# Softmax attention loop of a three-block transformer step: probabilities scaled before the transpose, values stationary, output written transposed

## What is computed

```python
def causal_attention_blocks(q, k, v):        # q, k: (1, 8, 256, 96), v: (1, 8, 256, 64); Q_BLOCK = 128
    for i in range(S // Q_BLOCK):
        s = jnp.einsum('bhqd,bhkd->bhqk', q[:, :, lo:hi], k[:, :, :hi])
        p = jax.nn.softmax(jnp.where(mask, s, -jnp.inf), axis=-1)
        outs.append(jnp.einsum('bhqk,bhkd->bhqd', p, v[:, :, :hi]))

o = jnp.concatenate([o_mla, o_moba], axis=-1)  # (1, 256, 1024)
x = x + o @ w_o
x = x + sq_relu_mlp(rms_norm_2(x, ffn_norm_g[layer]), w_ff1[layer], w_ff2[layer])
```

## Time and profile before

| | us |
|---|---|
| median of 3 runs (lowest, highest) | 868.62 (868.02, 869.25) |
| span of the profiled execution, first to last instruction | 866.2 |
| what lies around the span, against the median of the runs | 2.4 |
| TensorE busy | 851.7 (98%) |
| VectorE busy | 591.9 (68%) |
| ScalarE busy | 441.4 (51%) |
| GpSimd busy | 117.3 (14%) |

### The profile page before, as it was taken

The page is one execution under the profiler, slowest core; times in us unless marked ns, Lnnn a source line. Parts: engine busy times, 40 slices in busy tenths (PEclk is TensorE's granted clock), DMA queues, the critical chain, the costliest instruction groups (busy, mean ns, idle before and its releaser), DMA issues.

```text
span 866.2 us, 13480 instructions
## 1 busy us (share of the span) xinstructions
PE 851.7 (98%) x5659; PEld 737.0 (85%) x5659; DVE 591.9 (68%) x738; ACT 441.4 (51%) x591; POOL 117.3 (14%) x74
## 2 busy tenths in 40 slices
PE   8999999999999999999999999999989999999998
PEld 7887888888788887888988889997868999999996
DVE  5684677666756678888788788786975655555553
ACT  6644466556953656754553446443164644444441
POOL 0100001111000004123144344540000000000000
PEclk9999999999999999999999999999999999999999
DMA  9927645555004436226455565556976465555621
GB/s 332 372 75 246 239 146 196 194 194 184 11 22 154 160 98 244 97 97 210 157 198 167 207 231 195 209 190 140 282 265 235 151 210 182 188 190 194 194 98 48
DMA packets 68405, 155.96 MB, mean 180 GB/s; under 512 B 3145, under 2 KB 6954, under 8 KB 68346
## 3 DMA queue, kind: packets, MB, share of 16 engines
q1 hardware_dynamic: 65312, 146.80, 50.1%
q0 software_dynamic: 2224, 7.67, 2.6%
q10 hardware_dynamic: 810, 0.63, 0.5%
HBM read 146.70 MB, written 7.34 MB: 178 GB/s over the span
## 4 chain that ended last, share of the span: by engine, by line
PE 91%; DVE 6%; ACT 2%; issue 1%; DMA 0%; ACTq 0%; DVEq 0%
PE bank L735 19%; PE bank L736 19%; PE bank L737 19%; PE bank L1062 7%; PE bank L1064 7%; PE bank L1060 7%; PE bank L728 3%; PE bank L844 2%; PE bank L834 1%; PE bank L946 1%; PE bank L885 1%; DVE pT L1826 1%; PE bank L1133 1%; PE bank L1122 1%; DMA vrows<-in_vecs 0%
## 5 line engine op out<-in xcount | busy, mean ns | idle before, releaser
L1725 DVE TENSOR_TENSOR wlo<-ring,whi 128x2048 fp32r<-128x2048 f32 (+1 forms) x103 | 251.7, 2449 | 135.3 <-ACT whi L1334 135.0
L1334 ACT ACTIVATE whi<-ring 128x2048 fp32r<-128x2048 f32 (+1 forms) x104 | 198.4, 1909 | 208.3 <-PE bank L737 143.2
L735 PE MATMUL bank<-whi,hT 128*128 128x512 f32 (+1 forms) x512 | 201.6, 394 | 3.2 <-DVE wlo L1955 1.4
L737 PE MATMUL bank<-whi,hT 128*128 128x512 f32 (+1 forms) x512 | 198.8, 388 | 0.0
L736 PE MATMUL bank<-wlo,hT 128*128 128x512 f32 (+1 forms) x512 | 198.7, 388 | 0.0
L1060 PE MATMUL bank<-hT,whi 128*128 128x256 f32 x512 | 145.3, 284 | 0.0
L1062 PE MATMUL bank<-hT,whi 128*128 128x256 f32 x512 | 144.9, 283 | 0.0
L1064 PE MATMUL bank<-hT,wlo 128*128 128x256 f32 x512 | 144.8, 283 | 0.0
L735 PEld LDWEIGHTS bank<-whi,hT 128*128 128x128 f32 x512 | 96.1, 188 | 25.0 <-issue 2.7
L737 PEld LDWEIGHTS bank<-whi,hT 128*128 128x128 f32 x512 | 96.1, 188 | 19.6
L736 PEld LDWEIGHTS bank<-wlo,hT 128*128 128x128 f32 x512 | 96.2, 188 | 19.0 <-issue 0.5
(11 more groups left out here) (296 smaller groups left out, 1026.9 us busy)
## 6 DMA issues: line engine op xcount, KB each, us to landing
ring<-in_w_ff SPq DMA_DIRECT2D x64, 1024.0 KB, 5.3
ring<-in_ple_gate_w SPq DMA_DIRECT2D x8, 1024.0 KB, 5.0
ring<-in_w_kv SPq DMA_DIRECT2D x8, 1024.0 KB, 5.0
ring<-in_b_w_in SPq DMA_DIRECT2D x8, 1024.0 KB, 5.0
ring<-in_a_w_in SPq DMA_DIRECT2D x7, 1024.0 KB, 13.1
ring<-in_w_in SPq DMA_DIRECT2D x6, 1024.0 KB, 5.8
ring<-in_w_glu SPq DMA_DIRECT2D x6, 1024.0 KB, 10.1
ring<-in_a_w_out SPq DMA_DIRECT2D x4, 1024.0 KB, 5.7
```

The lines of the kernel that those rows point to most:

```text
L735: pe.matmul(bank_cols, high[:, at[0], at[1]], w_high, start=first, stop=False)
L737: return pe.matmul(bank_cols, low[:, at[0], at[1]], w_high, start=False, stop=last)
L1334: act.activation(whi[at], raw_rows(g), ACT.Copy).then_inc(high_made, 1)
L1725: dve.tensor_tensor(wlo[at], raw_rows(g), whi[at], ALU.subtract).then_inc(low_made, 1)
```

## The change

The reciprocals move into the loop, head by head, on VectorE. GpSimd multiplies the probabilities of a head, in place, by the reciprocal of each row's denominator (two instructions a head), and the transposes wait for that in place of the exponential. The value products take the values as the stationary operand (64 columns) and the transposed probabilities as the moving one, for two heads at a time, one in the lower and one in the upper 64 partitions of the output, so that the output is already transposed: two heads give one chunk of 128 rows and 256 token columns. A unit `("T", "o2", m)` holds two such chunks. `soft_out`, `h` as its target and the 16 transposes of `h` go; ScalarE and VectorE take the units out inside the loop where they are ready. The four `o2` units name their banks (6 and 7) and no longer draw from the rotation.

```diff
 def plan():
     soft_plan(u)
-    turned_in_two(u, "o2")
     rolled(u, "w_o", ("ffn", 0), "v")
 def soft_plan(u):
         if i > AHEAD and (i - AHEAD - 1) % 4 == 3:
             m = (i - AHEAD - 1) // 4
-            u.add(("soft_out", m), "v", bank=6 + m % 2)
+            u.add(("T", "o2", m), "av", bank=6 + m % 2)
...
+    for m in range(3):
+        u.freed_in_order([("probsT", 4 * m + 5), ("probsT", 4 * m + 6), ("T", "o2", m)])
 # TensorE
             def probs_turned(n):
                 b = begin(("probsT", n))
-                emptied(("scores", n))
+                pe.wait_ge(probs_scaled, 2 * n + 2)
...
-            def soft_values(n):
-                name = ("soft_out", n // 4)
-                b = begin(name) if n % 4 == 0 else bank(name)
-                o = b[:, (n % 4) * P:(n % 4) * P + P]
-                emptied(("probsT", n))
-                a = probsT[:, n % 3, :]
-                vh = (vm if n < MH else vb)[:, :, n % MH * HD:(n % MH + 1) * HD]
-                pe.matmul(o[:, 0:HD], a[:, 0:P], vh[:, 0, :], start=True, stop=True)
-                pe.matmul(o[:, HD:P], a[:, P:S], vh[:, 0, :], start=True, stop=False)
-                last = pe.matmul(o[:, HD:P], a[:, S:S + P], vh[:, 1, :], start=False, stop=True)
-                if n % 4 == 3:
+            def soft_values(c):
+                name = ("T", "o2", c // 2)
+                b = begin(name) if c % 2 == 0 else bank(name)
+                at = S * (c % 2)
+                for n in (2 * c, 2 * c + 1):
+                    emptied(("probsT", n))
+                sides = []
+                for odd in range(2):
+                    n = 2 * c + odd
+                    vh = (vm if n < MH else vb)[:, :, n % MH * HD:(n % MH + 1) * HD]
+                    sides.append((b[HD * odd:HD * odd + HD, at:at + S], vh, probsT[:, n % 3, :]))
+                for o, vh, a in sides:
+                    pe.matmul(o, vh[:, 0, :], a[:, 0:S], start=True, stop=False, skip_group_check=True)
+                for o, vh, a in sides:
+                    last = pe.matmul(o[:, P:S], vh[:, 1, :], a[:, S:384], start=False, stop=True, skip_group_check=True)
+                if c % 2:
                     last.then_inc(pe_done, 1)
...
-                if i > AHEAD:
-                    soft_values(i - AHEAD - 1)
+                if i > AHEAD and (i - AHEAD) % 2 == 0:
+                    soft_values((i - AHEAD) // 2 - 1)
...
-            turn("o2", h, ready=lambda k: emptied(("soft_out", k)))
 # ScalarE, in the loop and behind it
+                if i in (8, 12):
+                    turned_high("o2", None, (i // 4 - 2,))
-            turned_high("o2", None)
+            turned_high("o2", None, (2, 3))
 # VectorE
-            def soft_out(m):
...
+            def reciprocals(i):
+                n, head = divmod(i, MH)
+                emptied(("scores", i))
+                dve.reciprocal(rden[:, n, head, :], den[:, n, head, :]).then_inc(rden_ready, 1)
...
-                if i > AHEAD and (i - AHEAD - 1) % 4 == 3:
-                    soft_out((i - AHEAD - 1) // 4)
+                if 0 < i <= 2 * MH:
+                    reciprocals(i - 1)
+                if i in (9, 13, 17):
+                    turned_low("o2", None, ((i - 9) // 4,))
                 if MH + 2 <= i < MH + 6:
                     refill_piece("wv", 0, i - MH - 2)
-            turned_low("o2", None)
+            turned_low("o2", None, (3,))
 # GpSimd
-            pool.wait_ge(pe_done, done(("soft_out", 3)))
+            for i in range(2 * MH):
+                n, head = divmod(i, MH)
+                pool.wait_ge(rden_ready, i + 1)
+                for t, cols in enumerate((slice(0, P), slice(P, 384))):
+                    a = probs[:, i % 3, cols]
+                    pool.tensor_scalar(a, a, rden[:, n, head, t:t + 1], None, ALU.mult).then_inc(probs_scaled, 1)
+            pool.wait_ge(pe_done, done(("T", "o2", 3)))
```

More of the change, by code:

```diff
@@ L486, in program @@
         sp_high, sp_low = sem("sp_high"), sem("sp_low")
+        rden_ready, probs_scaled = sem("rden_ready"), sem("probs_scaled")
         hid_made, hid_high, hid_low = sem("hid_made"), sem("hid_high"), sem("hid_low")
```

## The result

The changed kernel takes **872.77 us** (median of 6 runs, 871.11 to 876.56) against 868.09 for the kernel before, measured beside it: a ratio of 1.0057 [1.0038, 1.0076]. The forecast was 868.5 with a range of 866.9 to 870.3. The profiled execution took 873.95 us with a span of 872.2. In three of the six executions TensorE's mean granted clock was 1.000 and they took 871.11 to 871.59; the other three had 0.998 to 0.993 and took 873.95 to 876.56, so part of the loss comes and goes from one execution to the next.

A forecast was written before the change was run, and what follows sets the result against it. It took TensorE as the kernel's bound, with VectorE about equal in the loop's second half. Terms of -1.1 (loop) and +1.0 (bank) gave a span of 866.1 and a time of 868.5 us, range 866.9 to 870.3.

The forecast's parts named there:

- The bank wait: Layer 0's first hidden product waits for VectorE's addition to x, as the bank rotation shifts by four: 1.0 us lost.
- The tail: From head 15's copy to the first w_o product: about 1.6 us in place of 3.51, 1.9 less.
- The value pair: TensorE's value products for two heads, with column halves overlapping: 0.95 us a pair.
- rival 4: Column halves of the value products don't overlap on TensorE: +0.8 us, 869.3; chance 0.10.
- The reciprocals of a head: Two-column reciprocals added to VectorE in the loop: about 0.08 us each, nine of them 0.7 us.
- The pieces of wlo: VectorE's four wlo pieces in the loop, 0.60 us each; over 0.7 would show the forecast wrong.
- rival 2: VectorE loses the SBUF port to GpSimd, four wlo pieces growing about 0.4 us each: 870.1; chance 0.15.
- the price of GpSimd's scaling: One head's scaling in the softmax loop, two instructions over 384 columns: 1.0 us, bounds 0.6 to 1.85.
- Rival 1: GpSimd's scaling becomes the loop's bound, from 1.8 us a head; 870.5 at 1.85; chance 0.13.
- the walk: Step-by-step tracing of the softmax loop's chain across engines: first w_o product at about 385.7, 1.1 us earlier.
- the first half: Heads 0 to 7, paced by bank 7 and ScalarE: no gain, scores of head 8 at 367.1 against 367.01.
- The sum: Loop's -1.1 and the bank's +1.0 added to the old span of 866.2: -0.1 us, 866.1.

The follow-up runs named there:

- c2: Changed kernel with the bank rotation of before and ten long-met TensorE waits a head in the loop: 869.58 us, 1.0014 of the kernel before.
- a1: Changed kernel with the bank rotation moved on by four behind the softmax loop, giving later units their old banks: 870.68 us, 1.0035 of the kernel before.
- c1: Changed kernel with scaling shared among GpSimd, VectorE and ScalarE, the banks of before and nine long-met waits a head: 867.63 us, 0.9995 of the kernel before.
- b4: Changed kernel with GpSimd scaling only the 256-column part, normalization of the other 128 columns left out: one run, 875.75 us.
- b1: Kernel before with 240 long-met TensorE waits added in the k, v and q products: 870.22 us, 1.0021 of the unpadded kernel before.
- c3: Changed kernel with scaling shared among GpSimd, VectorE and ScalarE and the banks of before, no padding waits: 870.87 us, 1.0031 of the kernel before.
- a2: Changed kernel with 192 long-met waits in the k, v and q products, restoring TensorE's stream length: 872.51 us, 1.0048 of the kernel before.
- a3: Changed kernel with the banks of before and 192 long-met waits in the k, v and q products: 870.87 us, 1.0029 of the kernel before.
- b2: Changed kernel with the banks of before and seven long-met waits ahead of each head's transposes: 870.50 us, 1.0023 of the kernel before.

## Why the prediction was wrong

**The number.** The loop and the banks alone would give about 870.2 us (868.1, 1.1 by c2 and 1.0 by a1's rows), against 868.5 forecast and just inside the range. What carries the time beyond the range arose in the S5 stage. So two steps failed, and both are named below.

**The steps that held.** The bank wait: +1.0 forecast, +1.02 seen, 0.97 given back in a1, from the rotation alone. The tail: 1.6 us from the last copy to the product forecast, 1.50 seen (386.64 to 388.14). The value pair: 0.95 forecast, 0.80 seen, so rival 4 (no overlap of the column halves) is false; for the end only the last pair counts, 0.15 us cheaper. The reciprocals of a head: 0.08 forecast, 0.07 to 0.08 seen (373.65 to 373.73). The pieces of wlo, for which over 0.7 us was named as a refutation, take 0.67 to 0.69: rival 2, that VectorE loses the port, is false. GpSimd loses: 1.80 us a head beside the pieces, 1.49 elsewhere, 1.2 us for four heads. The reason given for it, that each piece starts ahead of the scaling, holds for two of the four. The second and the fourth piece start at 375.38 and 379.62, while records of GpSimd that began at 374.85 and 379.34 still run to 375.77 and 379.94; they take 0.67 and 0.69 us all the same, and it is GpSimd's next record that grows (0.77 in place of 0.60, 1.18 in place of 0.92). The Trainium skill (SBUF — State Buffer, Who interferes with whom) says that whoever starts first blocks the other; by the starts in this trace, which are rough on GpSimd, that doesn't come out: VectorE kept its pace in either order.

**The first step that failed: the price of GpSimd's scaling.** "1.0 us a head", from the one-input copy at 1.62 ns a column. It measured 1.49, and 1.6 with what the port takes; a pair far from 1.0 was among the signs that the forecast named for being wrong. The transposes of heads 1 and 2 came at 359.76 and 362.34, not at 358.9 and 361.1. The view by form of the changed kernel (instructions | busy us, mean ns of one | idle before):

```profile
L2405 POOL TENSOR_SCALAR aux<-aux,rden 128x256 f32<-128x256 f32 x16 | 15.0, 937 | 0.0
...
L2405 POOL TENSOR_SCALAR aux<-aux,rden 128x128 f32<-128x128 f32 x16 | 10.5, 658 | 4.3 <-DVE rden L2223 4.1
L2436 POOL TENSOR_TENSOR aux<-pa,cs 128x1152 f32<-128x1152 f32 x4 | 10.5, 2621 | 66.9 <-PE bank L1070 66.9
```

These means hold the four heads beside the pieces. Away from them the two records of a head take 0.60 and 0.92 us. The second 128 columns thus cost 0.32 us, 2.5 ns a column, and some 0.28 us is left to start a record. For 384 columns and two starts that is 0.96 and 0.56 us, where the forecast had 0.62 and 0.38 with the semaphores: both parts were too small, the columns by twice as much as the starts. The product of two tensors in the third row has 2.3 ns a column with its start (2621 over 1152). The bounds of the prediction, 0.6 to 1.85, held the truth, but the value was taken at the wrong row: the pace of the scaling is that of two tensors. It reads a scalar for each partition besides the tensor; that this is the reason was not tested. The Trainium skill (GPSIMD Engine Reference, Engine selection) says that against VectorE one input is roughly at line rate and two are about twice as slow. For two tensors the rows agree, 2.3 ns a column against 1.1 of VectorE's subtraction (2.28 us for 2048). The scaling, with one tensor, doesn't go at VectorE's rate: in c1 GpSimd takes 737 ns for 128 columns and VectorE 287.

**Rival 1 was the right one, with its threshold misplaced.** It was given 0.13, as GpSimd would need 1.8 us a head to set the end, from "356.4 + 16R + 1.6". That line leaves out GpSimd's own waits. By the timeline: 356.62, 16 times 1.49 is 23.8, its five waits for reciprocals 4.2, the port 1.2: 385.8, and the last record ends at 385.94. With waits and port in the line, the copy of head 15 (0.7 us behind GpSimd's end, 385.94 to 386.64) leaves the forecast 384.1 when 356.6 + 16R + 5.4 passes 383.4: from R = 1.3 on, as an estimate with the waits left as they are. Three points show the dependence: with 0, 0.99 and 1.6 us a head (the means by form) the loop takes 32.31, 32.95 and 35.38 us. Below 1.0 another wait covers most; from there to 1.6 each 0.1 us costs 0.4 on average, which fits a flat part up to some 1.3 and a steep one behind it, though no point lies between. The middle point, at the price that the forecast used, is 33.2 forecast and 32.95 seen: the walk was right and the term was mis-sized, and with it the first half ("no gain"): the scores of head 8 were forecast at 367.1, 14.6 behind the first scores, and came at 368.25, 15.5 behind; in b4 they come 14.53 behind, without scaling 14.42.

**The second step that failed: the sum.** It added the two differences to the old span and took all that follows as rigid, with no reason given. The S5 stage is not. Of 6.0 us between the profiled executions 3.39 arose there, and of 4.7 between the medians about 2.6 are left after the loop (1.1 by c2) and the banks (1.0 by a1's rows). No rival named it. That the length of TensorE's stream alone makes the stalls is shown by b1 (stalls without the change), by c3 against c1 (3.2 us between the same work) and by the places of all 16 stalls.

**What stays open.** The places of the stalls tie them to the packets; why a packet starts late at some lengths of the stream and not at others is not shown. Load on the DMA engines alone is not enough: it is 0.88 to 0.92 in the windows of the changed kernel above, and 0.84 to 1.06 from 609 to 634 us in the kernel before, which has no stall. Why the clock falls behind some stalls and not behind that of 2 us in b1, and why c3 loses it in six runs of twelve, is open. Nor is it shown why a2's median lies above its parts.

## What to carry to other kernels

Price GpSimd's multiplication by a per-partition scalar by its two-input rows and not by its copy, with a start for each instruction, and when it stands in a loop count its own waits into the point from which it is the bound. When a change removes units from a rotation of banks, follow the rotation to the first unit with a named bank. In a stage of many short products like this one, a change in the number of TensorE's instructions can move a microsecond or more far behind the edit: compare the stages that the edit doesn't touch, and repeat with a stream padded to its old length before a difference under half a per cent is put down to the edit.

## What the runs showed of the hardware

- **Where instruction packets fall matters.** Stalls with no semaphore of 0.2 to 3.2 us in the S5 stage, 16 in eight kernels, all at places of TensorE's stream that lie multiples of 256 records apart, each ending 2.3 to 2.8 us after the start of a 16 KB packet; none in the profiled executions of before, a2, a3, c1 and c2. One of up to 1.8 us can be hidden by a wait that was there already (b2).
- **The clock can fall within a busy stage.** After the stall of 2.05 us the granted clock was at 1.2 GHz for 3.4 us (0.66 in the window) and came back; in b4 in two stretches of 6.8 us each (0.71 and 0.76 in windows of 10 us). In b1 a stall of 2.01 us was followed by no fall.
- **A wait that was met long ago isn't free on a full TensorE.** 192 (a2) and 240 (b1) ahead of products that run back to back stand as 96 records each and cost 1.1 and 1.2 us, 0.012 us a record; 112 to 160 in the loop, where TensorE waits for others, cost nothing that shows (35.42 to 35.45 us).
- **The same scaling on three engines** (by form, c1, mean ns): GpSimd takes 2.6 times VectorE's time for 128 columns and twice ScalarE's for 256.

```profile
L2425 POOL TENSOR_SCALAR aux<-aux,rden 128x256 f32<-128x256 f32 x8 | 8.0, 1004 | 6.7 <-DVE rden L2239 6.7
L2425 POOL TENSOR_SCALAR aux<-aux,rden 128x128 f32<-128x128 f32 x8 | 5.9, 737 | 6.4 <-DVE rden L2239 6.4
L1547 ACT ACTIVATE aux<-aux,rden 128x256 f32<-128x256 f32 x8 | 4.1, 506 | 0.2 <-DVE rden L2239 0.2
L2243 DVE TENSOR_SCALAR aux<-aux,rden 128x128 f32<-128x128 f32 x8 | 2.3, 287 | 0.3
```
